# Rotary embedding of a 16-head attention by exchange of partition groups on VectorE, without permutation products

## The reference

```python
qa, ka, va, qb, kb, vb = _split(h @ w_in, AB_SIZES)
qa = apply_rope(rms_norm(qa.reshape(B, S, 8, 64), g_qa), ang_2d)
ka = apply_rope(rms_norm(ka.reshape(B, S, 2, 64), g_ka), ang_2d)
oa = blocked_dense_attention(qa, ka, va, 64 ** -0.5)
qb = apply_rope(qb.reshape(B, S, 8, 64), ang_1d)
kb = apply_rope(kb.reshape(B, S, 2, 64), ang_1d)
ob = window_attention_with_sink(qb, kb, vb, sink, 64 ** -0.5)
return jnp.concatenate([oa, ob], axis=-1) @ w_out

def apply_rope(x, ang):
    cos, sin = jnp.cos(ang), jnp.sin(ang)
    x1, x2 = jnp.split(x, 2, axis=-1)
    return jnp.concatenate([x1 * cos - x2 * sin, x1 * sin + x2 * cos], axis=-1)
```

## Time and profile before

| | |
|---|---|
| median of 3 runs | 2259.08 us (2258.82 to 2262.1) |
| span of the profiled execution | 2258.2 us |
| TensorE busy | 2233.8 us (99%) |
| VectorE busy | 1334.5 us (59%) |
| ScalarE busy | 1048.2 us (46%) |
| GpSimd busy | 265.1 us (12%) |

### The profile page before, as it was taken

How to read it: one execution, slowest core, us unless ns; L and a number is a source line. 1 busy time by engine, 2 the same in 40 slices (tenths; PEclk the granted TensorE clock), 3 DMA queues, 4 the chain that set the end, 5 groups by cost and what they waited for, 6 DMA issues and landing times.

```text
span 2258.2 us, 35046 instructions
## 1 busy us (share of the span) xinstructions
PE 2233.8 (99%) x14526; PEld 1967.2 (87%) x14526; DVE 1334.5 (59%) x2541; ACT 1048.2 (46%) x2002; POOL 265.1 (12%) x298
## 2 busy tenths in 40 slices
PE   8999999999999999999999999999999999999998
PEld 7888878999978888888899999999988888988887
DVE  6654523567754223457565776547777876667875
ACT  5543422345452322354443555445366554466553
POOL 0000000312201012100002221120210110120110
PEclk9999999999999999999999999999999999999999
DMA  7522134221134222234333223446524555324554
GB/s 311 199 88 88 63 149 169 76 76 66 67 112 149 75 75 93 84 131 152 129 134 137 85 94 113 168 150 226 150 94 150 189 180 184 136 94 141 195 171 147
DMA packets 54958, 298.61 MB, mean 132 GB/s; under 512 B 9280, under 2 KB 15680, under 8 KB 23504
## 3 DMA queue, kind: packets, MB, share of 16 engines
q1 hardware_dynamic: 52464, 292.15, 36.7%
q10 hardware_dynamic: 2336, 4.23, 0.8%
HBM read 293.18 MB, written 3.44 MB: 131 GB/s over the span
## 4 chain that ended last, share of the span: by engine, by line
PE 92%; DVE 4%; ACT 2%; DMA 1%; issue 0%; ACTq 0%; SPq 0%; DVEq 0%
PE PS L629 89%; PE PS L633 4%; DVE TM L2504 1%; ACT TM L1737 1%; DVE wl L2523 1%; ACT TMG L1737 0%; DMA raw<-in_wpk 0%; DVE colS L2512 0%; DMA Y<-factors_d 0%; ACT wh L1747 0%; DVE wl L2525 0%; DVE HY L2512 0%; DVE TM L2673 0%; DVE TMG L2512 0%; DVE colS L3081 0%
## 5 line engine op out<-in xcount | busy, mean ns | idle before, releaser
L629 PE MATMUL PS<-HY,wh 128*128 128x512 f32 (+3 forms) x4944 | 1280.5, 342 | 7.6 <-DVE wl L2523 3.6
L629 PEld LDWEIGHTS PS<-HY,wh 128*128 128x128 f32 (+2 forms) x4944 | 848.0, 189 | 123.7 <-issue 12.0
L629 PE MATMUL PS<-HY,wl 128*128 128x256 f32 (+1 forms) x3000 | 923.8, 308 | 0.0
L629 PEld LDWEIGHTS PS<-HY,wl 128*128 128x128 f32 x3000 | 566.4, 189 | 30.1
L2523 DVE TENSOR_TENSOR wl<-raw,wh 128x1280 fp32r<-128x1280 f32 (+1 forms) x238 | 345.7, 1452 | 410.0 <-ACT wh L1747 409.9
L629 PE MATMUL PS<-wh,HY 128*128 128x256 f32 (+1 forms) x2468 | 526.5, 306 | 0.2
L1737 ACT ACTIVATE TM<-PS 128x512 f32<-128x512 f32 (+5 forms) x407 | 198.6, 502 | 545.4 <-PE PS L629 428.1
L629 PEld LDWEIGHTS PS<-wh,HY 128*128 128x128 f32 x2468 | 404.8, 191 | 19.5 <-ACT TM L1737 0.8
L1747 ACT ACTIVATE wh<-raw 128x1280 fp32r<-128x1280 f32 (+2 forms) x246 | 295.7, 1202 | 259.2 <-PE PS L629 177.7
L629 PE MATMUL PS<-wl,HY 128*128 128x256 f32 (+1 forms) x1234 | 373.0, 302 | 0.0
L2525 DVE TENSOR_TENSOR wl<-raw,wh 128x768 fp32r<-128x768 f32 (+1 forms) x238 | 246.8, 1037 | 0.0
(11 more groups left out here) (194 smaller groups left out, 1737.9 us busy)
## 6 DMA issues: line engine op xcount, KB each, us to landing
raw<-in_wpk SPq DMA_DIRECT2D x233, 1024.0 KB, 4.8
raw<-in_wpk SPq DMA_DIRECT2D x32, 704.0 KB, 4.1
TM<-in_wpk SPq DMA_DIRECT2D x6, 1024.0 KB, 16.5
Y<-factors_d ACTq DMA_DIRECT2D x16, 256.0 KB, 5.2
X<-in_xin SPq DMA_DIRECT2D x1, 2048.0 KB, 15.0
Y<-in_wpk SPq DMA_DIRECT2D x2, 1024.0 KB, 20.3
Y<-bias_d SPq DMA_DIRECT2D x4, 512.0 KB, 10.2
raw<-in_wpk SPq DMA_DIRECT2D x3, 512.0 KB, 3.7
```

Of the source, the lines that this page charges most:

```text
L629: return P.x.matmul(o, l, r, start=start, stop=stop)
```

## The change

The permutation products go. VectorE forms the rotated half directly: each of four groups of 32 partitions of the scratch tile is the neighbouring group of the source times the sines, with the sign as the scalar of the instruction. GpSimd multiplies the source by the cosines into the destination (not in place), in one instruction for both blocks, as soon as the source is there, and in the order k0, k1, q0, q1, q2, q3. VectorE then adds its scratch tile to the destination in one instruction. The rotary of q2 moves on VectorE from ahead of `heads` to behind the first two heads, that of q3 from there to behind heads 2 and 3. TensorE's waits for the rotary steps of k0, k1, q0, q2 and q3 ahead of the products and the first transposes go; the waits of the scores remain.

```diff
@@ tensor_program, self_attention @@
                         if c == 0 and i == 1:
-                            rope("ab_k0", kraw[:, 0:1], 1, perm2, 128, 7, (dve_step, "ab_k0_norm"))
-                            rope("ab_k1", kraw[:, 1:2], 1, perm2, 128, 5, (dve_step, "ab_k"))
+                            P.wait_ge(dve_step, "ab_k0_norm")
...
-                    if i == 2:
-                        rope("ab_q0", tm(2560, [2, 256]), 2, perm2, 128, 4, (dve_step, ("ab_q_norm", 0)))
...
-                P.wait_ge(dve_step, "ab_k0_rope")
-                rope("ab_q1", tm(3072, [2, 256]), 2, perm2, 128, 7, (dve_step, ("ab_q_norm", 1)))
-                P.wait_ge(dve_step, "ab_k1_rope")
-                rope("ab_q2", tm(3584, [2, 256]), 2, perm2, 128, 5, (dve_step, ("ab_q", 2)))
-                P.wait_ge(dve_step, "ab_q0_rope")
-                rope("ab_q3", tm(4096, [2, 256]), 2, perm2, 128, 4, (dve_step, ("ab_q", 3)))
...
-                heads(("ab", 0), 16, qf, kf, vf, ofun, lambda h: None,
-                      lambda h: P.wait_ge(dve_step, ("ab_q3_rope", "ab_q2_rope")[h]), ofree, need, last_values)
+                heads(("ab", 0), 16, qf, kf, vf, ofun, lambda h: None, lambda h: None, ofree, need, last_values)
@@ vector_program @@
+            def turned_halves(key, dst, src, n, table):
+
+                D.wait_own(dve_step)
+                for b in range(4):
+                    o, i = slice(32 * b, 32 * b + 32), slice(32 * (b ^ 1), 32 * (b ^ 1) + 32)
+                    sines = table[i, 1].unsqueeze(1).to_broadcast([32, n, 256])
+                    stt(tB[o, 0:n], src[i, 0:n], 1.0 if b % 2 else -1.0, sines, ALU.mult, ALU.mult)
+                D.wait_own(dve_step)
+                D.wait_ge(pool_step, key)
+                tt(dst[:, 0:n], dst[:, 0:n], tB[:, 0:n], ALU.add, key + "_rope")
...
-                        rope("ab_k0", K[:, 0:1], kraw[:, 0:1], 1, rope2d, 128, 7)
+                        turned_halves("ab_k0", K[:, 0:1], kraw[:, 0:1], 1, rope2d)
                         D.wait_ge(pe_step, ("ab_q_spread", 0))
                         x0 = tm(2560, [512])
                         tt(x0, x0, bank(6), ALU.mult, ("ab_q_norm", 0))
-                        rope("ab_k1", K[:, 1:2], kraw[:, 1:2], 1, rope1d, 128, 5)
+                        turned_halves("ab_k1", K[:, 1:2], kraw[:, 1:2], 1, rope1d)
...
-                        rope("ab_q0", Q[:, 0:2], tm(2560, [2, 256]), 2, rope2d, 128, 4)
+                        turned_halves("ab_q0", Q[:, 0:2], tm(2560, [2, 256]), 2, rope2d)
...
-                rope("ab_q1", Q[:, 2:4], tm(3072, [2, 256]), 2, rope2d, 128, 7)
-                rope("ab_q2", QB[:, 0:2], tm(3584, [2, 256]), 2, rope1d, 128, 5)
+                turned_halves("ab_q1", Q[:, 2:4], tm(3072, [2, 256]), 2, rope2d)
 
                 def between(s):
                     if s == 0:
-                        rope("ab_q3", QB[:, 2:4], tm(4096, [2, 256]), 2, rope1d, 128, 4)
+                        turned_halves("ab_q2", QB[:, 0:2], tm(3584, [2, 256]), 2, rope1d)
+                    if s == 1:
+                        turned_halves("ab_q3", QB[:, 2:4], tm(4096, [2, 256]), 2, rope1d)
@@ pool_program @@
+            def cosines(key, dst, src, n, table, after):
+
+                G.wait_ge(dve_step, after)
+                tt(dst, src, table[:, 0].unsqueeze(1).to_broadcast([128, n, 256]), ALU.mult, key)
...
+                    cosines("ab_k0", K[:, 0:1], kraw[:, 0:1], 1, rope2d, "ab_k0_norm")
+                    cosines("ab_k1", K[:, 1:2], kraw[:, 1:2], 1, rope1d, "ab_k")
+                    cosines("ab_q0", Q[:, 0:2], tm(2560, [2, 256]), 2, rope2d, ("ab_q_norm", 0))
+                    cosines("ab_q1", Q[:, 2:4], tm(3072, [2, 256]), 2, rope2d, ("ab_q_norm", 1))
                     for j in range(2):
-                        rope(f"ab_q{2 + j}", tm(3584 + 512 * j, [2, 256]), 2, rope1d, 128)
+                        cosines(f"ab_q{2 + j}", QB[:, 2 * j:2 * j + 2], tm(3584 + 512 * j, [2, 256]), 2, rope1d, ("ab_q", 2 + j))
```

## The result

| | before | after |
|---|---|---|
| median of the runs | 2261.51 us (2258.82 to 2263.64, 5 runs) | 2268.61 us (2267.74 to 2272.31, 5 runs) |
| span of the profiled execution | 2258.2 us | 2266.5 us (its own time 2268.31) |

The ratio is 1.004 [1.003, 1.0051]: slower by 7.1 us between the medians, by 8.3 us between the spans. The forecast's base of 2259.08 is the median of the first three of before's five runs. The forecast was 2265.3, with a range up to 2268.0: the direction was right, the loss larger than forecast, and the time 0.6 us outside the range.

The account below looks back on a forecast made before the run. TensorE was taken to bound the kernel overall, VectorE the stretch from the first scores. First scores +1.85 and head stretch +4.39 made +6.2 us; on 2259.1 that gave 2265.3 us, range 2260.7 to 2268.0.

Parts of the forecast that it names:

- the two waits: TensorE's waits on VectorE at the q norms' spread (1613.82) and first scores (1626.24): rotary work hidden, but cover thin.
- the hold between partition groups: VectorE's rotary products: each held for its new start partition, stepping 0.70 us at 512 columns, 0.44 at 256.
- Rival 2: GpSimd hold-up, but VectorE's products run without a hold: +4.5, 2263.6 us; chance 0.17 including part of the hold-ups.
- rival 3: VectorE's additions fit, 32-partition products taking about a quarter: about 2255.5 us; chance 0.08 together with no change.
- GpSimd's hold-ups: GpSimd's cosine products keep VectorE out 1.14 us each: one beside k1's products, three beside q1's.
- Rival 1: No hold-up of VectorE by GpSimd: +1.7, 2260.8 us; chance 0.12.
- q1's sum: VectorE's rotary addition for q1 ahead of the first scores: 0.68 us, within 6.92 for q1's products and sum.
- T0: Start of the first scores, waiting for q1's rotary: 1628.1 against 1626.24, +1.85 us, TensorE idle for 4 us.
- S: VectorE's stretch from the reduction of head 0 to that of head 4: 11.66 us instead of 7.27, +4.4.
- the head stretch: VectorE from first reduction to that of heads 4 and 5, now with q2's and q3's calls: 11.66 us, +4.4.
- rival 4: Idle around the scores lets TensorE's clock fall, or further casts collide: 2268 us and above; chance 0.08.
- F: Start of the fifth pair of scores, before at about 1638.6: forecast 6 us later, the rest of the trace shifted.

Follow-up runs that it names:

- e4: Changed kernel with q1, q2 and q3 rotated as before, only k0, k1 and q0 the new way: 2261.92 us against 2263.45 before, ratio 0.9996.
- e5: Changed kernel with q0's four products all on partitions 0 to 31, into four tiles (q0 not rotated properly): 2268.57 us.
- h1: Kernel before with only q2 exchanged, in VectorE's idle, q3's rotary ahead of the heads, half a memory product moved: 2257.9 us against 2260.99, ratio 0.9991.
- e7: Changed kernel with all of TensorE's idle stretches in the stage filled with unread products: 2267.77 us against 2261.28 before, ratio 1.0028.
- e1: Changed kernel with unread TensorE products in two stretches, ahead of the first scores and first denominators: 2270.15 us against 2263.45 before, ratio 1.0032.
- e6: Kernel before with its ten permutation products cut from 256 columns to one, VectorE and GpSimd unchanged: 2260.55 us against 2261.28, ratio 0.9997.
- a1: The changed kernel itself, unaltered, profiled anew: 2269.26 us against 2260.99 before, ratio 1.0038.

## Why the prediction came out as it did

**Right: what bounds the kernel here, and the direction.** The cover at the two waits was as thin as said. The spread came at 1613.98 (forecast 1614.1), with idle ahead of it, and ate the first 1.72 us; e4 shows that in isolation. The first scores waited 4.56 us (forecast 4) and came at 1628.46 (forecast 1628.1).

**Right: the hold between partition groups.** Forecast 0.70 and 0.44 a step; measured 0.71 and 0.45, and e5 removes it. This is the rule of the Trainium skill, "VectorE: DVE Perf Modes", section "Two Vector instructions with no wait between them"; the trace and e5 agree with it. Rival 2 falls with it, and rival 3 with the full length of the products.

**Right in kind, off in size: GpSimd's hold-ups.** Forecast 1.14 each, one at k1 and three at q1; measured 1.00, and 0.97 each. So four hold-ups cost 3.91 instead of 4.56. Rival 1 (none) falls. By the Trainium skill's page "SBUF — State Buffer", section "Who interferes with whom", the shared port pair is an exclusive lock. GpSimd's product takes 1.29 where it starts first (h1), and VectorE lost 0.97 for each. So reckoning the lock with the whole of GpSimd's instruction gives too much for this pair of instructions, and the measurement decides.

**Missed: q1's sum beside the cast.** The sum for q1 was put at 0.68; it took 1.62, as GpSimd goes straight from its products to the cast at 1626.15. That is +0.93, and with the smaller hold-ups q1's call is 7.39 against 6.92. T0 became +2.22 on the clock of the trace, +2.29 from the common point, for +1.85. I had used that cast ahead of the scores to take 0.41 out of S, and hadn't asked what VectorE would be doing beside it.

**Mis-sized a little: the head stretch.** Forecast 11.66, measured 12.01, and 11.92 with the clock up. A pair of maxima up to the next product took 1.73, not 1.60: the call waits for VectorE's own last instruction, 0.13 each, twice. The rest of 12.01, 0.09, goes with the clock; most of it is the wait for the slow second pair.

**The step that failed: that TensorE's clock stays at its top level.** The sum had no term for it. It stood as rival 4, with 0.08, on the ground that "the clock stayed at 1.00 through 1.6 us of idle". But that row's 1.6 us are two idles, of 1.15 and 0.47 us, and the change makes idles of 1.88, 4.56 and 3.20 us, longer than either, and my own forecast had the 4 us in it. Nor does the clock of before never leave its top level, as I read from slices of some 56 us. A window of before in the first network shows a stretch at half clock, with TensorE shown busy throughout and for 14 us ahead of it:

```profile
984.00:988.00 4.00, 4.00 (x25) 3.80 (x28) 2.93 (x10) 1.09 (x3) 0.00 (x0) 0.57 0.46 195
```

After shows 0.51 and 0.56 in two stretches, and e7, with nothing but TensorE kept busy, gives 1.72 us back. With it: 6.24 forecast; +0.70 for VectorE's terms (6.94); +1.72 for the clock (8.66). Rival 4 was thus part of what happened, beside the forecast rather than in its place, and I treated them as alternatives. Its price, a microsecond for each at 1.2 GHz, was too high: from 1628.46 to 1632.40 TensorE worked for 3.94 us at half clock, and only the 0.94 of the first scores lay on VectorE's path.

**The base.** The sum stood on 2259.08, on the ground that a run's time is 0.9 us above its span. In each run for which both are on record it is about 1.8 above (2268.31 and 2266.5 for the profiled execution of after). So the span of 2258.2 belongs to a time of about 2260.0, and the same +6.2 would have given 2266.2. Of the 3.0 us from 2265.3 to 2268.31, some 0.9 are this term and 2.4 the stage; the span grew by 0.4 less than F. Without this error the time would have fallen inside the range, and so it would have without the clock's 1.72. On any base the loss at F was forecast 2.4 too small. Before ranged from 2259.0 to 2263.74 in one series of 21 runs.

**Open.** What decides whether an idle of 1.9 us brings a fall (e1) or none (after, e4) was not settled. Over all the traces, idles of 1.79 to 2.25 us stood ahead of a stretch at half clock in four places and ahead of none in ten. Nor was a form of the change tried in which GpSimd's casts too are moved, or one in which q2's call stays ahead of the heads, where before had q2's rotary. With the clock up VectorE stood idle for 1.22 us there, waiting for the first scores (e7). By an estimate from that row about 1.2 of the 6.94 us belong to this move and not to the exchange.

## What to carry to other kernels

- Work taken from the engine that is busy 99% of the time is worth nothing where that engine waits next for the one that gets the work. Find the next two waits and subtract their slack first: here 1.72 of 4.3 us were gone at once, and the rest was outweighed by VectorE's longer calls.
- A split by partition groups has the price of full instructions: four of 32 partitions cost four, and a hold on top. Use it only where VectorE is idle (h1), and keep GpSimd's work on SBUF out of that place.
- When a forecast contains an idle of TensorE, put the slower clock into the sum, at what lies right behind the idle; don't leave it to a rival.

## What the runs showed of the hardware

Twelve one-column passes of a float32 product take 1.39 us (e6), twelve of 256 columns 2.75: cutting 256 columns to one saves only about half.

The two traces of the changed kernel part at one place in the first network, far from the change. The timeline of TensorE in a1 there:

```profile
1039.00 0.65 PE L629 MATMUL PS<-HY,wh 128*128 128x256 f32 x2 [2.61 <-ACT TM L1727]
```

And in after:

```profile
1038.28 0.50 PE L629 MATMUL PS<-HY,wh 128*128 128x256 f32 x2 [1.27 <-ACT TM L1727]
```

The windows of a1 behind it, and that of after:

```profile
1040.00:1050.00 10.00, 10.00 (x66) 9.68 (x65) 6.50 (x10) 5.17 (x10) 0.00 (x0) 0.87 0.84 277
```

```profile
1040.00:1050.00 10.00, 10.00 (x73) 9.58 (x73) 6.54 (x9) 4.99 (x11) 0.00 (x0) 1.00 0.75 271
```

An idle of 2.61 us was followed by a clock of 0.87, one of 1.27 by 1.00. VectorE's instructions in a1 were 0.6 us ahead of those of after up to about 1032 us, 0.7 to 0.9 behind them from 1033 us on, with the longer idle, and 2.2 behind from 1060 us on. So the longer idle and the slower clock behind it come to 2.8 us, a third of the effect studied here, and a comparison of single traces has to be made from a common point close to the change.
